# Forgetting softmax: VectorE's half of each ScalarE pair a step behind, idle steps at the narrowest row tile

## The reference

```python
# first block (one layer)
proj = rmsnorm(x) @ w_in      # a_u a_v a_z | b_q b_fl b_i b_z | c_q c_k c_v c_z c_fl
y_a = gmlp(gelu(a_u), layernorm per group of gelu(a_v)) * silu(a_z)
y_b = hgrn2(b_q, b_fl, b_i) -> rmsnorm per head, * silu(b_z)
# forgetting attention, 8 heads of 64, causal, four query tiles of 128 rows:
for blk in range(4):          # q0 = 128*blk, q1 = q0 + 128
    s = q[q0:q1] @ k[:q1].T / 8 + c[q0:q1, None] - c[None, :q1]   # c: summed log forget gates
    p = softmax(where(causal, s, -inf));  o = p @ v[:q1]
y_c = o * silu(c_z)
x = x + concat(y_a, y_b, y_c) @ w_out
x = rmsnorm(x)
# then two layers: four mixers (mLSTM, grouped-query, neighbourhood and
# differential attention), gated merge, output projection, gated FFN
```

## Time and profile before

| | |
|---|---|
| time, median of 3 runs | 2735.52 us (2735.26 to 2735.67) |
| the profiled execution | 2737.32 us, its span 2735.5 us |
| mean granted TensorE clock | 0.983 of full speed |
| busy in the span | TensorE 2629.6 us (96%), weight loads 2202.4 us (81%), VectorE 1471.7 us (54%), ScalarE 1134.8 us (41%), GpSimd 40.2 us |

### The profile page before, as it was taken

One profiled execution on the slowest core, in us unless ns is written; L12 is line 12 of the kernel. 1 busy time (PEld: TensorE's weight loads), 2 busy tenths in 40 slices (PEclk: granted clock), 3 DMA queues, 4 the chain that ended last, 5 costly groups with the idle time before them and its releaser, 6 DMA issues. The chain is left out here.

```text
span 2735.5 us, 33990 instructions
## 1 busy us (share of the span) xinstructions
PE 2629.6 (96%) x13218; PEld 2202.4 (81%) x13218; DVE 1471.7 (54%) x2719; ACT 1134.8 (41%) x1946; POOL 40.2 (1%) x64
## 2 busy tenths in 40 slices
PE   7998879999999999999999899999999999999997
PEld 6887768788888888778888787888888887788886
DVE  5655548554545658544444566644456486444444
ACT  4435344433644647332222344335536374322222
POOL 0000000000000000000000000000001000000000
PEclk9998999999999999999999999999999999999999
DMA  4220123123213421223332232233134221233322
GB/s 138 86 61 20 62 62 86 55 71 99 68 55 89 81 85 60 72 83 96 98 99 93 70 93 62 62 92 83 45 91 77 90 68 62 85 100 93 100 77 100
DMA packets 118431, 216.98 MB, mean 79 GB/s; under 512 B 14272, under 2 KB 21824, under 8 KB 118272
## 3 DMA queue, kind: packets, MB, share of 16 engines
q1 hardware_dynamic: 114528, 201.97, 24.3%
q0 software_dynamic: 3744, 12.85, 3.0%
HBM read 212.69 MB, written 2.10 MB: 79 GB/s over the span
## 5 line engine op out<-in xcount | busy, mean ns | idle before, releaser
L1331 DVE TENSOR_TENSOR wL<-wraw,wH 128x1024 fp32r<-128x1024 f32 (+1 forms) x388 | 460.0, 1186 | 716.5 <-ACT wH L872 714.9
L872 ACT ACTIVATE wH<-wraw 128x1024 fp32r<-128x1024 f32 (+1 forms) x388 | 398.3, 1027 | 927.7 <-PE bank L537 499.9
L537 PE MATMUL bank<-wH,hH 128*128 128x512 f32 (+1 forms) x1248 | 501.2, 402 | 8.7 <-DVE wL L1331 3.7
L537 PE MATMUL bank<-wH,hL 128*128 128x512 f32 (+1 forms) x1248 | 479.9, 385 | 0.0
L537 PE MATMUL bank<-wL,hH 128*128 128x512 f32 (+1 forms) x1248 | 479.7, 384 | 0.0
L540 PE MATMUL bank<-hH,wH 128*128 128x512 f32 x1208 | 473.4, 392 | 3.2 <-ACT set L890 1.6
L540 PE MATMUL bank<-hH,wL 128*128 128x512 f32 x1208 | 470.4, 389 | 0.0
L540 PE MATMUL bank<-hL,wH 128*128 128x512 f32 x1208 | 470.2, 389 | 0.0
L537 PEld LDWEIGHTS bank<-wH,hH 128*128 128x128 f32 x1248 | 237.2, 190 | 62.2 <-issue 7.5
L537 PEld LDWEIGHTS bank<-wH,hL 128*128 128x128 f32 x1248 | 237.1, 190 | 48.5 <-issue 3.3
L537 PEld LDWEIGHTS bank<-wL,hH 128*128 128x128 f32 x1248 | 236.7, 190 | 47.9
(11 more groups left out here) (295 smaller groups left out, 2853.8 us busy)
## 6 DMA issues: line engine op xcount, KB each, us to landing
wraw<-in_w_in_dram SPq DMA_DIRECT2D x180, 512.0 KB, 3.6
wraw<-in_w_ffn_down_dram SPq DMA_DIRECT2D x44, 512.0 KB, 3.4
wraw<-in_w_ffn_gate_dram SPq DMA_DIRECT2D x40, 512.0 KB, 3.6
wraw<-in_w_ffn_up_dram SPq DMA_DIRECT2D x40, 512.0 KB, 3.6
wraw<-in_w_out_dram SPq DMA_DIRECT2D x24, 512.0 KB, 3.5
tab<-in_rpb_rev_dram POOLq DMA_DIRECT2D x32, 224.0 KB, 6.3
wraw<-in_w_up_a_dram SPq DMA_DIRECT2D x8, 512.0 KB, 3.4
wraw<-in_w_up_b_dram SPq DMA_DIRECT2D x8, 512.0 KB, 3.4
```

Source lines behind the costliest of these rows:

```text
L537: mm = pe.matmul(bank[t][:, 0:b.cols], act_part[:, k, t * P:(t + 1) * P], w_part[:, kk, :], start=first, stop=last)
L872: A(wH[:, u % W_SLOTS, 0:width], wraw[:, u % RAW_SLOTS, 0:width], ACT.Copy).then_inc(S["w_hi"], 1)
L1331: V.tensor_tensor(wL[:, u % W_SLOTS, 0:width], wraw[:, u % RAW_SLOTS, 0:width], wH[:, u % W_SLOTS, 0:width].bitcast(F32), ALU.subtract).th ...
```

## The change

- `FOX_IDLE` goes from the steps with row tile 3 to those with row tile 0. UV's unit 3 then ends in steps 11, 13, 14 and 15 instead of 10, 12, 13 and 14 (`uv_last`); AZ's unit 3 keeps steps 32 to 35 (`az_last`). The number of steps stays 36.
- In `gated_mlp` VectorE's cube comes one step after ScalarE's square, ScalarE's tanh two steps and VectorE's products three steps after it; VectorE's product for AZ comes one step after ScalarE's tanh, so VectorE's loop gets one step more. The normalisation steps move by the distances in the diff, to steps 19 (mean of v) to 30 (scaled o into `merged`), where they were 17 to 26.
- ScalarE's row split moves from s % 4 = 1 to s % 4 = 0, in the forgetting and in the differential softmax.
- `hgrn_out` takes chunk numbers; chunks 0 and 1 are issued after the first group of UV's unit 0, chunks 2 and 3 after the third.
- The transposes of columns 0 and 1 stand after the second group of O0's unit 2 instead of after its fourth.

```diff
@@ -226,7 +226,7 @@
 
 
 DIFF_IDLE = (1, 3, 17, 19)
-FOX_IDLE = (3, 7, 11, 15, 19, 23, 27, 31)
+FOX_IDLE = (0, 4, 8, 12, 16, 20, 24, 28)
 
 
 def lambda_init(l):
@@ -414,7 +414,9 @@
             return [(0, 4, 0), (64, 4, 4), (32, 4, 8), (96, 4, 12)]
 
         fox_side = side_groups([by_name[(0, "UV")], by_name[(0, "AZ")]], done=1, idle=FOX_IDLE)
-        uv_end = max(s for s, g in enumerate(fox_side) if g and g[0].name == "UV")
+        uv_last, az_last = ([s for s, g in enumerate(fox_side) if g and g[0].name == name and g[1] == 3]
+                            for name in ("UV", "AZ"))
+        uv_end = uv_last[-1]
 
         def bcast_rows(name_ap, n):
             return bass.AP(tensor=name_ap.tensor, offset=name_ap.offset, ap=[[0, P], [1, n]])
@@ -716,11 +718,11 @@
                         mm.then_inc(S["lvl_done"], 1)
                 return level
 
-            def hgrn_out():
+            def hgrn_out(*chunks):
 
 
                 pe.wait_ge(S["lvl_used"], 4 * (LEVELS + 1))
-                for m in range(NT):
+                for m in chunks:
                     if m >= 2:
                         pe.wait_ge(S["ho_read"], 2 * (m - 1))
                     tok = slice(m * P, (m + 1) * P)
@@ -750,8 +752,7 @@
             dense(0, "CK", each={(1, 3): hgrn_keys, (3, 1): hgrn_updates})
             dense(0, "CV", each={(i, 1): hgrn_level(i) for i in range(4)})
             dense(0, "CZ", each={(i, 1): hgrn_level(4 + i) for i in range(4)})
-            dense(0, "UV", stop=1)
-            hgrn_out()
+            dense(0, "UV", stop=1, each={(0, 0): lambda: hgrn_out(0, 1), (0, 2): lambda: hgrn_out(2, 3)})
             for name in ("CQ", "CK", "CV"):
                 evacuated(by_name[(0, name)])
             pe.wait_ge(S["masks_ready"], 1)
@@ -765,9 +766,7 @@
 
                 if i == 0:
                     gmlp()
-                elif i == 2:
-                    transposes(merged, (0, 1), "y_ready", 1)
-            dense(0, "O0", 6, gated_part)
+            dense(0, "O0", 6, gated_part, each={(2, 1): lambda: transposes(merged, (0, 1), "y_ready", 1)})
             dense(0, "O1")
 
 
@@ -1015,7 +1014,7 @@
                             act.wait_ge(S["pv_done"], y - 1)
                         A(sbufPT[:, y % 2, 0:it["kmax"]], bank[TP][:, 0:it["kmax"]], ACT.Copy).then_inc(S["ptev"], 1)
                     gates(side, s)
-                    if s % NT == 1 and NT < s < len(items) - NT:
+                    if s % NT == (0 if kind in ("fox", "diff") else 1) and NT <= s < len(items) - NT:
                         split_rows(items, s // NT + 1, q, k)
                     if kind == "diff" and 5 <= s < len(items) + 5 and weighs(items[s - 5]):
                         it, y = items[s - 5], nth_y[s - 5]
@@ -1096,7 +1095,7 @@
                     A(o_flat[:, m * 256:(m + 1) * 256].rearrange("p (g h d) -> p g h d", g=2, h=2)[:, :, half, :],
                       bank[SC + 2 * (m % 2) + half][:, 0:2 * DH].rearrange("p (g d) -> p g d", g=2),
                       ACT.Copy).then_inc(S["ho_read"], 1)
-            tanh_out[0] = gelu_tanh
+            tanh_out[0], tanh0 = gelu_tanh, len(taken)
 
             def gelu(b, t):
 
@@ -1109,28 +1108,26 @@
             def gated_mlp(s):
 
                 b, i, t = fox_side[s] if s < len(fox_side) and fox_side[s] else (by_name[(0, "UV")], -1, NT)
+                if s - 2 in uv_last:
+                    gelu(by_name[(0, "UV")], uv_last.index(s - 2))
                 if b.name == "UV" and i == 3:
                     ready(b, t)
                     if t >= 2:
-                        act.wait_ge(S["tanh_ready"], len(taken))
+                        act.wait_ge(S["tanh_ready"], tanh0 + t - 1)
                     else:
                         scratch_free()
                     A(cube[:, t % 2, :], bank[t][:, :], ACT.Square).then_inc(S["gsq"], 1)
-                    if t:
-                        gelu(b, t - 1)
-                if s == uv_end + 1:
-                    gelu(by_name[(0, "UV")], NT - 1)
                 if b.name == "AZ" and i == 3:
                     ready(b, t)
                     tanh_half(b, t, slice(0, 256))
                 if s == 1:
                     act.wait_ge(S["ho_read"], 2 * NT)
                     A(o_squared, o_flat, ACT.Square).then_inc(S["sq_ready"], 1)
-                elif s == uv_end + 4:
+                elif s == uv_end + 5:
                     act.wait_ge(S["ms_ready"], n("ms_ready", 2))
                     A(v_squared, vv, ACT.Square).then_inc(S["sq_ready"], 1)
                     n("sq_ready", 2)
-                elif s == uv_end + 6:
+                elif s == uv_end + 8:
                     act.wait_ge(S["ms_ready"], n("ms_ready"))
                     A(st32, st32, ACT.Sqrt).then_inc(S["sd_ready"], 1)
             softmax(fox_items(), fox_side, q2, k2, gated_mlp)
@@ -1460,7 +1457,7 @@
                 nth_y = y_numbers(items, n)
                 a0 = n.at("a_ready")
                 kind = items[0]["kind"]
-                for s in range(max(len(items) + 4, len(side))):
+                for s in range(max(len(items) + 4, len(side) + 1)):
                     if 4 <= s < len(items) + 4 and weighs(items[s - 4]):
                         it, y = items[s - 4], nth_y[s - 4]
                         w, r = it["v"][1], rs[:, y % 4:y % 4 + 1]
@@ -1747,51 +1744,50 @@
 
             def gated_mlp(s):
 
-                b, i, t = fox_side[s] if s < len(fox_side) and fox_side[s] else (by_name[(0, "UV")], -1, NT)
                 v_g, _, mean = per_group(v_f, v_f, st32c[:, 0:16], 16)
                 o_g, _, r_g = per_group(o_flat, o_flat, st32b[:, 0:16], 16)
-                if b.name == "UV" and i == 3:
+                if s - 1 in uv_last:
+                    t = uv_last.index(s - 1)
                     dve.wait_ge(S["gsq"], n("gsq"))
                     then(V.tensor_scalar(cube[:, t % 2, :], cube[:, t % 2, :], GELU_A, 1.0, ALU.mult, ALU.add))
                     V.tensor_tensor(cube[:, t % 2, :], cube[:, t % 2, :], bank[t][:, :], ALU.mult).then_inc(S["gin2"], 1)
-                    if t:
-                        gelu(t - 1)
-                if b.name == "AZ" and i == 3:
-                    silu(merged[:, t, 0:256], bank[t][:, 0:256], b, t)
-                if s == 2:
+                if s - 3 in uv_last:
+                    gelu(uv_last.index(s - 3))
+                if s - 1 in az_last:
+                    t = az_last.index(s - 1)
+                    silu(merged[:, t, 0:256], bank[t][:, 0:256], by_name[(0, "AZ")], t)
+                if s == 3:
                     dve.wait_ge(S["sq_ready"], n("sq_ready"))
                     group_sums(st32[:, 0:16], o_squared, 16)
                     V.tensor_scalar(st32[:, 0:16], st32[:, 0:16], 1.0 / DH, EPS, ALU.mult, ALU.add).then_inc(
                         S["ms_ready"], 1)
-                elif s == uv_end + 1:
-                    gelu(NT - 1)
-                elif s == uv_end + 3:
+                elif s == uv_end + 4:
                     for t in range(NT):
                         evacuated(by_name[(0, "UV")], t)
                     group_sums(st32c[:, 0:16], v_f, 16)
                     then(V.tensor_scalar(st32c[:, 0:16], st32c[:, 0:16], 1.0 / DH, None, ALU.mult))
                     V.tensor_tensor(v_g, v_g, mean, ALU.subtract).then_inc(S["ms_ready"], 1)
-                elif s == uv_end + 5:
+                elif s == uv_end + 7:
                     dve.wait_ge(S["sq_ready"], n("sq_ready"))
                     group_sums(st32[:, 16:32], v_squared, 16)
                     V.tensor_scalar(st32[:, 16:32], st32[:, 16:32], 1.0 / DH, 4 * EPS, ALU.mult, ALU.add).then_inc(
                         S["ms_ready"], 1)
-                elif s == uv_end + 7:
+                elif s == uv_end + 10:
                     dve.wait_ge(S["sd_ready"], n("sd_ready"))
                     then(V.reciprocal(st32b, st32))
                     then(V.tensor_tensor(v_g, v_g, st32b[:, 16:32].unsqueeze(2).to_broadcast([P, 16, DH]), ALU.mult))
-                elif s == uv_end + 8:
+                elif s == uv_end + 11:
                     dve.wait_ge(S["gp_step"], 16 * 4)
                     then(V.tensor_tensor(gflat[:, 0:512], gflat[:, 0:512], gflat[:, 1024:1536], ALU.mult))
                     then(V.tensor_tensor(vv, vv, gflat[:, 512:768].unsqueeze(1).to_broadcast([P, NT, 256]), ALU.mult))
-                elif s == uv_end + 9:
+                elif s == uv_end + 12:
                     V.tensor_tensor(vv, vv, gflat[:, 768:1024].unsqueeze(1).to_broadcast([P, NT, 256]),
                                     ALU.add).then_inc(S["vn_ready"], 1)
-                elif s == uv_end + 10:
+                elif s == uv_end + 13:
                     then(V.tensor_tensor(o_g, o_g, r_g, ALU.mult))
-                elif s == uv_end + 11:
+                elif s == uv_end + 14:
                     then(V.tensor_tensor(o_g, o_g, onorm.unsqueeze(1).to_broadcast([P, 16, DH]), ALU.mult))
```

(2 more changed lines are left out.)

## The result

| | before | changed |
|---|---|---|
| time, median | 2735.39 us (4 runs, 2734.07 to 2735.67) | 2711.41 us (4 runs, 2709.57 to 2716.00) |
| the profiled execution | 2737.32 us, span 2735.5 us | 2716.00 us, span 2714.2 us |

The ratio is 0.9916 (95% interval 0.9899 to 0.9933), 24.0 us of median faster; 22.3 us were forecast. The profiled execution is the slowest of the four and shows 21.3 us. The changed kernel scatters over 6.4 us here and the one before over 1.6, but in 25 further executions beside the first experiments the one before ran from 2731.7 to 2737.8.

The account below looks back on a forecast made before the run. With TensorE busy 96% of the span, only its waits and clock were left to gain. Parts A to F (4.4 + 10.5 + 3.0 + 0.8 + 1.6 + 2.0) gave 22.3 us: 2713.2 us, 8-in-10 range 2704 to 2727.

Parts of the forecast that it names:

- Part A: HGRN output inside projection UV: ScalarE copy wait goes, less time at half clock; gain 4.4 us (1.0 to 6.4).
- Part B: Forgetting softmax steps 4 to 15: waits go and clock mostly recovers; gain 10.5 us (4.4 to 12.6).
- Part C: Forgetting softmax steps 16 to 31: VectorE's work bunched, waits about as many as now; gain 3.0 us (-6 to +8).
- Part D: Softmax steps 32 to 35: VectorE's wait behind ScalarE's tanh for AZ goes; gain 0.8 us (0 to 2.3).
- Part E: O0: earlier transposes of columns 0 and 1 cover the 1.57 us wait; gain 1.6 us (0 to 1.6).
- Part F: Differential softmax, both layers: earlier ScalarE row split removes four score waits; gain 2.0 us (-2 to +3.2).
- 1 (clock as bad): TensorE spends as long at 1.2 GHz as now, only waits are gained: 9 us, 2726.5 us; chance 0.17.
- 2 (bunching): Bunching in steps 16 to 31 costs more, a loss of 6 there: 12 us gained, 2723.5 us; chance 0.12.
- 3: Clock stays up nearly throughout, steps 16 to 31 gaining 6: 30 us gained, 2705.5 us; chance 0.10.
- 4 (ScalarE's early split slows): Earlier row split delays exponentials and transposes in three softmaxes: 34 us cost against 22, 2747 us; chance 0.03.
- 5 (the waits only change places): Waits only move elsewhere: gain under 0.2%, 2732 us; chance 0.04.
- signs of being wrong: Half-clock spells inside the softmax still adding to over 20 us, or waits on ScalarE exceeding those on VectorE.

Follow-up runs that it names:

- e1: Kernel before with only the HGRN output in two pairs of chunks inside UV's unit 0: ratio 0.9981, 5.2 us faster (2.7 to 7.7).
- e5: Changed kernel with the HGRN output again in one piece behind UV's unit 0: 2717.2 us, 5.8 us over the changed kernel, executions overlapping.
- e6: Changed kernel with ScalarE's row split of the forgetting softmax back at s % 4 = 1: 2715.0 us, 3.6 us over the changed kernel, overlapping ratios.
- e7: Changed kernel with FOX_IDLE back at row tile 3 (wide idle steps): 2712.2 us, 0.8 us over the changed kernel, not distinguishable from nothing.
- e9: Changed kernel with idle steps 0, 4, 8, 12, 16 narrow and 23, 27, 31 wide: 2709.8 us, 1.6 us under the changed kernel, intervals overlapping.
- e8: Changed kernel with ScalarE's copy ahead of its exponential in row-tile-3 steps of the forgetting softmax: 2711.6 us, no gain.
- e10: e9 with the normalisation of v and scaling of o two steps later: 2703.9 us, 5.9 us under e9, 7.5 us under the changed kernel.
- e4: Kernel before with only the gated MLP's halves a step behind and the later normalisation steps; idle steps wide: 15.3 us faster (11.2 to 19.4).
- e3: Kernel before with only FOX_IDLE moved to row tile 0: no difference (1.6 us faster to 3.6 us slower).
- e2: Kernel before with only the differential softmax's row split a step earlier and O0's transposes of columns 0 and 1 earlier: ratio 0.9980, 5.5 us faster.
- e12: e9 with the HGRN output in three pieces, behind UV's first, second and third groups: 2710.6 us, no difference from e9.

## Why the prediction was right, step by step

The sum came nearer than its parts. In the profiled execution A to F gained 0.75, 12.85, 0.43, 1.51, 1.86 and 3.9 us, where 4.4, 10.5, 3.0, 0.8, 1.6 and 2.0 were reckoned: A and C fell short by 6.2 us, the others brought 5.2 more than reckoned, and 21.3 stands against 22.3. That these misses cancel is luck; that the waits went where the prediction said is not.

**Part A** (4.4 us): right in the median, by e1 (5.2 us, 2.7 to 7.7) and less surely e5 (5.8 us), and wrong for the one profiled execution, which gained 0.75 us before step 4. The 1.05 us wait went. Over the seven profiles with the order in two pieces (changed, e1, e6, e7, e9, e8, e10: 13.7, 6.8, 6.8, 10.2, 3.4, 3.4, 13.7 us at half before step 4), the mean is 8.3 us against 13.7 to 17.1 us with one piece, and step 4 starts 3.1 us earlier in the mean. I had taken the clock at one value; it is a spread. I had also expected the fall near the end of the second pair; in the changed kernel the first fall, at 188.9 us, struck the wide groups behind the first pair, 4.4 us after the first narrow product, as before. The sign that I had named, the clock at 1.00 at 195 us, was met there by 0.6 us only; the second fall came at 195.6.

**Part B** (10.5 us): the mechanism held, its size was 12.85. The 2.1 us that I held back, 0.5 for step 14 and 1.6 for a half-clock spell, were not needed: no wait and no spell from step 4 to 15, the bound of 12.6 us reached. Step 14 was long on VectorE, as I had reckoned, but its idle neighbour is step 16, and the wait came there and in step 17 (0.57 us for ScalarE's copy and 0.77 us for VectorE). Part of the excess may be the execution that it is read against: the same code took 40.2 us in e1. What I had not divided is who does it: the step-behind halves give about 8.7 us (42.9 to 34.2, e4), the idle steps by themselves 3.7 or less (e3), and beside the halves the early row split brings 1.9 us with wide idle steps (32.3, e7), the narrow idle steps 4.1 us without it (30.1, e6), and both together no more (30.0).

**Part C** (3.0 us): 0.43 us, inside the bounds, but the sixteen steps took 48.4 us and the sign was 44 to 47. The waits behind the bunching were read rightly: over steps 14 to 20 they are 4.2 us for 4.4 reckoned (0.57, 0.77 and 0.77 at 16, 17 and 19, 2.1 at 20), step 25 waits 1.53 us behind the square root for 2 reckoned, and all of them come to 9.0 for 10. "About as many as now" was a wrong reading, as the kernel before has 6.9 us of waits there: the change adds 2.1 us of waits to this stretch, and only the clock paid for them. The mis-sized term is the clock: I allowed 3.5 us for one spell of 6.8 us, and there were three, 13.6 us; beyond the waits and the 32.3 us of work the stretch has 7.1 us (9.6 before; 1.3 in e10, which has no half-clock spell there). And the place is where the change's title costs: with wide idle steps the same stretch takes 44.0 us (e7), spread out it takes 38.7 (e10). VectorE's and ScalarE's total was never the bound, the bunching was.

**Part D** 1.51 us for 0.8: the copy's wait of 0.87 us behind a weight split, which was to remain, is gone as well; with wide idle steps it is still there (e7). **Part E**: 1.86 us for 1.6; the wait of the earlier trace rows is gone. **Part F** (2.0 us): about 3.9 us on the traces. The four waits of the earlier trace rows, 3.2 us, are gone. Of the rest a part at least is the execution and not the edit: behind the softmax the changed kernel has 47.3 us at half clock for 50.5, and e1 and e4, which lack parts E and F, are 1.5 and 1.6 us shorter there too. I halved this term for a push on ScalarE's exponentials that no run shows.

**Rivals.** 1 (clock as bad) fell: 27.3 us at half from the HGRN output to step 31 against 44.2. 2 (bunching) was half true, as a term of part C. 3 was not reached, but e10 shows that its part C was to be had. 4 (ScalarE's early split slows) is refuted: by e2 for the differential softmax, and by e6 for the forgetting one, where undoing it brings no gain. 5 (the waits only change places) holds for steps 16 to 31 alone. Of the signs of being wrong neither showed: 13.6 us at half inside the softmax, and 4.7 us of waits on ScalarE against 5.2 on VectorE, the second by little. That the drain of the Trainium skill (ScalarE: Activation LUTs, What ACT_TABLE_LOAD costs) would take part C's gain away is not borne out: the wait behind the square root was 1.53 us, and in the changed kernel too the loads and the square root follow each other at once (timeline of ScalarE). The gain of part C went nearly all the same, by the clock.

```profile
266.84 1.28 ACT L1132 ACT_TABLE_LOAD   x1
268.14 0.23 ACT L1132 ACTIVATE small<-small 128x32 f32<-128x32 f32 x1
268.38 1.28 ACT L1008 ACT_TABLE_LOAD   x1
```

## What to carry to other kernels

Put work that needs another engine's result into a later step than the one that makes it; with the later normalisation that comes with it, this was two thirds of the gain here, and moving the gaps where TensorE has nothing to issue was nothing. A short wait can cost more than its length: the waits taken away in steps 4 to 15 were about 8 us, and the clock that came back with them another 4 to 5. Once the halves are apart, look at the sum of the helper's work per step: two long steps in a row ahead of a gap are waited for even where the total fits, and spreading them gave 6 us more (e9 to e10). When a stage is divided into parts, let both kernels have issued the same work at each boundary, and compare a stretch that was not changed, to see what one execution's figure is worth.

## What the runs showed of the hardware

The granted clock differs between executions of one order of instructions: before step 4 it was at 1.2 GHz for 3.4 to 13.7 us in seven profiles with the HGRN output in two pieces, for 13.7 us in four with it in one piece and 17.1 us in e3. TensorE had not waited before any of these falls. The clock can also fall at the start of wide products that stand behind narrow ones (188.9 us in the changed kernel), which then take 0.63 us instead of 0.39 (timeline of TensorE, changed kernel):

```profile
188.40 0.39 PE L539 MATMUL bank<-wH,hL 128*128 128x512 f32 x1
...
188.89 0.63 PE L539 MATMUL bank<-wH,hH 128*128 128x512 f32 x1
```

What makes it fall there stays open: e12 rules out one reason and names none. It is not shown that a kernel with fewer waits scatters more: the changed kernel ran from 2709.6 to 2716.0 us, the one before from 2731.7 to 2737.8 in 25 executions.
